# Eight phases of a three-block kernel: where the dense slots lie that TensorE takes ahead across a phase edge

## What is computed

```
x = first_block(x, ...)    # short convolution, sparse attention (16 heads), gated mlp; three gated branches
x = second_block(x, ...)   # stick-breaking, indexed sparse and differential attention; then a feed-forward
x = third_block(x, ...)    # decayed ("forgetting") attention, gated linear recurrence, convolution; feed-forward

g_i = sigmoid(h @ w_in[gate columns i]);  term = g_i * (ys[i] @ w_br[i])      # first block, three branches
p   = masked_softmax(s);  o = p @ v                                            # attention, per head
attn = einsum('bhtk,bhsk,bhtsk->bhts', q, k, decay);  o = attn @ v + (q * exp(b)) @ state   # recurrence, third block
```

## The kernel before

| phase | line | lanes beside the dense one | dense slots, of which led |
|---|---|---|---|
| 1 | 1808 | sparse attention of the first block | 64, 16 |
| 2 | 2781 | stick-breaking attention, key search | 280, 16 |
| 3 | 2792 | head norms, bias tables | 96, 16 |
| 4 | 2819 | attention of the second block | 224, 16 |
| 5 | 2846 | head norm, cuts into halves | 48, 16 |
| 6 | 3564 | recurrence (`Hgrn`) | 96, 16 |
| 7 | 3583 | five norm and gate lanes | 64, 16 |
| 8 | 3607 | attention of the third block, cuts | 56, 16 |

## Time and profile before

### The profile page before, as it was taken

One profiled execution on the slowest core, in us unless ns is written; L12 is line 12 of the kernel. 1 busy time (PEld: TensorE's weight loads), 2 busy tenths in 40 slices (PEclk: granted clock), 3 DMA queues, 4 the chain that ended last, 5 costly groups with the idle time before them and its releaser, 6 DMA issues. The chain is left out here.

```text
span 3029.7 us, 40331 instructions
## 1 busy us (share of the span) xinstructions
PE 2888.8 (95%) x16205; PEld 2351.3 (78%) x16205; DVE 1361.9 (45%) x2458; ACT 1139.7 (38%) x2067; POOL 1237.1 (41%) x593
## 2 busy tenths in 40 slices
PE   6999999999999979999998999999998999999998
PEld 4875557888888867777787999988787757888887
DVE  5427651342043332773542555542477643566620
ACT  4347662222244333443553422222343355432221
POOL 5432214444444532222121545554444422545553
PEclk9989999999999988999997999999999999999999
DMA  7410002222322211113222422223222222422232
GB/s 261 140 49 15 15 29 98 92 97 97 115 94 98 93 47 62 42 42 93 70 84 88 144 85 91 96 98 107 84 92 86 86 73 99 158 95 92 99 102 90
DMA packets 83457, 272.70 MB, mean 90 GB/s; under 512 B 9863, under 2 KB 10119, under 8 KB 83144
## 3 DMA queue, kind: packets, MB, share of 16 engines
q1 hardware_dynamic: 81936, 269.23, 26.9%
q10 hardware_dynamic: 1336, 0.89, 0.1%
HBM read 255.34 MB, written 14.75 MB: 89 GB/s over the span
## 5 line engine op out<-in xcount | busy, mean ns | idle before, releaser
L131 POOL TENSOR_TENSOR weights_lo<-weights_raw,weights_hi 128x1024 fp32r<-128x1024 f32 x415 | 1007.7, 2430 | 1323.9 <-ACT weights_hi L123 1323.7
L123 ACT ACTIVATE weights_hi<-weights_raw 128x1024 fp32r<-128x1024 f32 x415 | 437.7, 1058 | 1049.9 <-PE acc L473 549.1
L471 PE MATMUL acc<-h_hi,weights_hi 128*128 128x512 f32 (+2 forms) x1808 | 665.9, 368 | 25.8 <-POOL h_lo L1350 6.7
L472 PE MATMUL acc<-h_lo,weights_hi 128*128 128x512 f32 (+2 forms) x1808 | 640.0, 354 | 0.0
L473 PE MATMUL acc<-h_hi,weights_lo 128*128 128x512 f32 (+2 forms) x1808 | 639.8, 354 | 0.0
L471 PEld LDWEIGHTS acc<-h_hi,weights_hi 128*128 128x128 f32 x1808 | 346.3, 192 | 106.1 <-issue 52.7
L473 PEld LDWEIGHTS acc<-h_hi,weights_lo 128*128 128x128 f32 x1808 | 346.6, 192 | 45.8
L472 PEld LDWEIGHTS acc<-h_lo,weights_hi 128*128 128x128 f32 x1808 | 347.3, 192 | 41.6 <-issue 0.2
L517 PE MATMUL acc<-weights_hi,h_hi 128*128 128x256 f32 (+1 forms) x480 | 144.8, 302 | 8.0 <-DVE h_lo L979 5.2
L471 PE MATMUL acc<-y_hi,weights_hi 128*128 128x512 f32 (+2 forms) x392 | 142.0, 362 | 10.0 <-DVE full L2725 5.3
L807 ACT ACTIVATE probs<-probs,low 128x31 f32<-128x31 f32 (+5 forms) x276 | 138.5, 503 | 23.1 <-DVE low L774 22.5
(11 more groups left out here) (436 smaller groups left out, 5267.0 us busy)
## 6 DMA issues: line engine op xcount, KB each, us to landing
weights_raw<-in_stream SPq DMA_DIRECT2D x415, 512.0 KB, 3.4
weight_ring<-in_w_ada SPq DMA_DIRECT2D x24, 512.5 KB, 7.5
gates<-gate_tiles SPq DMA_DIRECT2D x24, 258.0 KB, 4.3
gate<-gates SPq DMA_DIRECT2D x8, 774.0 KB, 7.4
held<-gates SPq DMA_DIRECT2D x8, 768.0 KB, 6.4
gates<-gate_tiles SPq DMA_DIRECT2D x23, 256.0 KB, 4.2
flipped<-bias_rows SPq DMA_DIRECT2D x8, 320.0 KB, 4.4
x<-in_x SPq DMA_DIRECT2D x2, 1024.0 KB, 13.9
```

Source lines behind the costliest of these rows:

```text
L123: act.activation(self.hi[:, at % CUT, :], self.raw[:, at % RAW, :], ACT.Copy).then_inc(self.hi_done, 1)
L131: pool.tensor_tensor(self.lo[:, at % CUT, :], self.raw[:, at % RAW, :], self.hi[:, at % CUT, :].bitcast(F32), ALU.subtract).then_inc(self. ...
L471: pe.matmul(out, left[0], right[0], start=start, stop=False)
L472: pe.matmul(out, left[0], right[1], start=False, stop=False)
```

## The change

A new function gives the dense lane a begin below zero, so that the marks of the led slots all lie before 0 and the remaining ones lie evenly from 0 to 1. Eight calls of `paced` use it; nothing else is edited.

```diff
+def ahead(dense, lead):
+
+    first = sum(dense.weights[:lead])
+    return -first / (sum(dense.weights) - first)
...
-            run.lanes(paced((dense.weights, 0, 1), (attention.weights, 0, 1)), [dense, attention], 2 * KT)
+            run.lanes(paced((dense.weights, ahead(dense, 2 * KT), 1), (attention.weights, 0, 1)), [dense, attention], 2 * KT)
...
-                run.lanes(paced((dense.weights, 0, 1), (heads.weights, 0, 1), ([1], 1, 1)), [dense, heads, StoredGates(store)], 2 * KT)
+                run.lanes(paced((dense.weights, ahead(dense, 2 * KT), 1), (heads.weights, 0, 1), ([1], 1, 1)), [dense, heads, StoredGates(store)], 2 * KT)
```

More of the change, by code:

```diff
@@ L2780, in second_attention @@
                 top = TopKeys(sem, sbuf, psum, k, early, penalty)
-                run.lanes(paced((dense.weights, 0, 1), (stick.weights, 0, 1), (top.weights, 0, 1)), [dense, stick, top], 2 * KT)
+                run.lanes(paced((dense.weights, ahead(dense, 2 * KT), 1), (stick.weights, 0, 1), (top.weights, 0, 1)), [dense, stick, top], 2 * KT)
         table = keep("table", [P, 8, TAB])
@@ L2791, in second_attention @@
                             HD, n, w, gains=(bias.scaled, 2))
-            run.lanes(paced((dense.weights, 0, 1), (norm.weights, 0, 1), (bias.weights, 0, 1), ([1], 1, 1)), [dense, norm, bias, StoredGates(store)], 2 * KT)
+            run.lanes(paced((dense.weights, ahead(dense, 2 * KT), 1), (norm.weights, 0, 1), (bias.weights, 0, 1), ([1], 1, 1)), [dense, norm, bias, StoredGates(store)], 2 * KT)
         groups = []
@@ L2818, in second_attention @@
             attention = PairAttend(sem, sbuf, psum, k, groups, True, T2)
-            run.lanes(paced((dense.weights, 0, 1), (attention.weights, 0, 1), ([1], 1, 1)), [dense, attention, StoredGates(store)], 2 * KT)
+            run.lanes(paced((dense.weights, ahead(dense, 2 * KT), 1), (attention.weights, 0, 1), ([1], 1, 1)), [dense, attention, StoredGates(store)], 2 * KT)
 GATES_A, GATES_B, GATES_C = 6, 14, 3
@@ L2845, in second_block @@
             cut = Cut(sem, [(qm[:, t, OUT:], *cuts.tile(t, T_OUT), (lambda act, t=t: act.wait_ge(scaled.done, t - DF_Q + 1)) if t >= DF_Q else None) for t in range(KT)])
-            run.lanes(paced((dense.weights, 0, 1), (scaled.weights, 0, 0.8), (cut.weights, 0, 1), ([1], 1, 1)),
+            run.lanes(paced((dense.weights, ahead(dense, 2 * KT), 1), (scaled.weights, 0, 0.8), (cut.weights, 0, 1), ([1], 1, 1)),
                       [dense, scaled, cut, StoredGates(store)], 2 * KT)
@@ L3582, in third_mixer @@
             gated = GateHeads(sem, hq, silu, both)
-            run.lanes(paced((dense.weights, 0, 1), (forget.weights, 0, 0.8), (fox_norm.weights, 0, 0.9), (head_norm.weights, 0, 0.75),
+            run.lanes(paced((dense.weights, ahead(dense, 2 * KT), 1), (forget.weights, 0, 0.8), (fox_norm.weights, 0, 0.9), (head_norm.weights, 0, 0.75),
                                 (conv_norm.weights, 0, 1), (gated.weights, 0.8, 1), ([1], 1, 1)),
@@ L3606, in third_mixer @@
                       + [(fox[:, FQ + pair, :], *cuts.tile(pair, S), lambda act, pair=pair: act.wait_ge(attention.out_read, len(groups) - pairs + pair + 1)) for pair in range(pairs)])
-            order = paced((dense.weights, 0, 1), (attention.weights, 0, 1), ([1] * (HG + CONV_TILES), 0.2, 0.8), ([1], 1, 1))
+            order = paced((dense.weights, ahead(dense, 2 * KT), 1), (attention.weights, 0, 1), ([1] * (HG + CONV_TILES), 0.2, 0.8), ([1], 1, 1))
             order = [2 if lane == 2 else lane for lane in order]
```

## The result

| | us |
|---|---|
| kernel before, median of 5 runs (range) | 3026.6 (3023.0 to 3031.1) |
| changed kernel, median of 5 runs (range) | 3042.4 (3036.9 to 3045.4) |
| ratio, 95% interval | 1.0054 (1.0043 to 1.0065) |
| profiled execution of the changed kernel, its span | 3043.4, 3041.6 |

The change makes the kernel slower by 16 us (13 to 20 by the interval). The forecast was 3004.0 with a range of 2986 to 3021: wrong in sign, and outside the range.

The account below looks back on a forecast made before the run. TensorE, busy for 2888.8 of 3029.7 us, bounds the kernel; time can come only from its 140.9 idle us or slow work. Eight phase terms sum to -23.0 us: 3026.9 - 23.0 = 3003.9, range 2986 to 3021.

Parts of the forecast that it names:

- rival C: Second half of phase 2: three waits, longer by the thinning, each bring a clock fall; +30 us, 3034 us; chance 0.07.
- rival D: Cover only moves: VectorE and ScalarE pace phases 2, 6, 7, 8, slots go missing later; -0.5 us, 3026 us; chance 0.12.
- Phase 1, -6: Start of phase 1: dense slots in the first gaps keep the clock from falling; -6 us, bounds 0 and 8.5.
- Phase 2, +1: Start of phase 2 gains 1 us, its fall stays; thinner end exposes 2 us of waits; +1, bounds -9 to +4.
- Phase 3, -0.7: Dense slots in phase 3 cover 0.7 of 2.8 us of waits for squares; bounds -2.8 and +1.
- Phase 4, -6.5: Phase 4: three waits of 1.9 us vanish, as does the 10.2 us fall behind them, taken as 4.6; -6.5 us.
- Phase 5, -4: Middle of phase 5: ScalarE's take moves ahead of the norm's chain, seven more slots done, clock still falls; -4 us.
- Phase 6, -2: Phase 6: more dense slots done early gain 5.8 us, later thinning gives back 3.9; -2 us, bounds +2.4 and -5.8.
- Phases 7 and 8, -3 and -1.8: Slots ahead of each item cover waits, 3.5 us for squares and 2.4 for scores, less small losses; -3 and -1.8 us.
- The signs: What would refute the forecast: clocks at 0.50 at phase ends, or phases 2 and 6 growing.

Follow-up runs that it names:

- the best choice of orders alone: Phases 1, 4 and 5 of the kernel before put in the new order, the other five left in the old one; 3018.5 us, ratio 0.9984.

## Why the prediction was wrong

The sum of the eight terms was -23; it came to +12 by the profiles and +16 by the times.

**The failed step** that turned the sign is the same in phases 2, 3 and 6: the thinner cover was priced as waiting time only. For phase 2 the prediction let 2 us of waits appear in the thinner tail and left the clock to fall as it did; for phases 3 and 6 it did not speak of the clock at all. In fact the waits in sum hardly grew (TensorE's idle time even fell by 3.1 us), and what grew is the time at half clock behind them: 47.8 us instead of 27.3 in phase 2, 10.2 instead of 0 in phase 3, 13.7 instead of 6.8 in phase 6. By the means of the profiles, at 0.43 us each, that cost 8.1, 1.8 and 2.5 us. The prediction had the mechanism in hand, in rival C, and gave it 0.07. Its condition, falls as long as the one at the start, was too strict: falls of 3 to 17 us in the second half of the phase were enough, and other phases joined.

**A second step** is as large in sum: gains were counted that did not come or that a later part of the phase took back. From -23 to +12 are 35 us, of which the clock in these three phases makes 12. Phases 4, 5, 7 and 8 make another 15: forecast -15.3, measured +0.1. That cover moved forward is missing later is rival D, which got 0.12; D and C together are what came.

- **Phase 1, -6.** Direction right; -5.2 over all profiles. But it has two parts. The prediction took the fall of 17.0 us in the earlier trace rows, and the slow first round of the earlier trace rows, for a property of the old order. Only two of seven profiles have it: without it the first round ends its last weighing at 217.52 instead of 224.74, and four of seven profiles look so. What the order itself brings is 3.4 us, mostly covered waits (TensorE's idle time 13.5 instead of 16.4), in the middle of the phase and not at its start. That it holds the clock where the old order sometimes does not is right: at most 3.4 us of half clock in six profiles.
- **Phase 2, +1.** Measured +10 to +12, beyond the upper bound of +4. Both parts lose, the new start 7 us and the new tail 3. At the start the prediction counted a microsecond of gain; the waits did shrink from 4.0 to 2.0 us, and the fall grew by 3.4.
- **Phase 3, -0.7** (the heading of that term says -1, the sum takes 0.7). +0.6 without a fall and +5.2 with one. The three waits for squares shrank from 2.8 to 1.8 us as said, but ScalarE's rounding and take delayed its later steps by 3.7 us, and a wait of 2.1 us for the table took the place of one of 0.3. Upper bound +1: missed by the fall.
- **Phase 4, -6.5.** -1.9. The three waits went and the start held its clock in all profiles, as said, but other waits came, and TensorE is idle for 3.3 us instead of 2.8. The rest of the phase gave back some 4 us of the gain. The fall in the tail is not the reason: it is 13.7 or 17.1 us long in the new order and 6.8 to 17.1 in the old one. At an even clock the phase became 1.9 us longer, with five more runs of dense slots; what of it is theirs stays open.
- **Phase 5, -4.** -2.6 in the profile, -1.3 over all, since the old order held its clock for most of the phase once (31.8 us). ScalarE's wait went and one for the norm's low part took its place, as said; it is 2.3 us long, so the clock still fell.
- **Phase 6, -2.** +4.4, beyond +2.4. The first pair product behind the low part came at 2305.79, 17.5 us into the phase, where 16.9 were expected: the rounding, the table load and the exponential lie as worked out. What went wrong comes next. A low part of GpSimd runs beside VectorE and slows it, which the prediction, counting GpSimd's moved steps "at nothing beyond that", had left out:

```profile
2303.80 2.96 POOL L3150 TENSOR_TENSOR k_part<-hf,decay 128x512 f32<-128x512 f32 x2 [0.71 <-ACT decay L3127]
...
2309.36 2.81 POOL L131 TENSOR_TENSOR weights_lo<-weights_raw,weights_hi 128x1024 fp32r<-128x1024 f32 x1
...
2309.88 2.84 DVE L3205 TENSOR_TENSOR kd<-kd,hf 128x512 f32<-128x512 f32 x1
...
2314.14 1.78 PE L3055 MATMUL pair_acc<-q_part,k_part 128*128 128x128 f32 x8 [3.49 <-DVE q_part L3193]
```

These are GpSimd, VectorE and TensorE of the changed kernel in phase 6. The low part that moved ahead of k_part cost nothing (k_part waited for ScalarE's decay). The next one did: the update of kd beside it takes 2.84 us, where it took 0.68, and TensorE waits 3.49. But the kernel before has such a meeting too, later in the chain, where TensorE waited 0.71:

```profile
2308.05 2.56 POOL L131 TENSOR_TENSOR weights_lo<-weights_raw,weights_hi 128x1024 fp32r<-128x1024 f32 x1
...
2308.30 2.86 DVE L3187 TENSOR_TENSOR q_part<-held,decay 128x512 f32<-128x512 f32 x1
```

Over the phase VectorE is busy for 100.5 instead of 97.4 us with the same 140 instructions. How much of the miss this is, no run isolates. The fifth item of the recurrence came 6.4 us later, with 13 slots more done, a gain of 2.6 and not 5.8; the thinner rest then cost 7, where 3.9 was allowed, some 4 of it by 10.2 us at half clock.
- **Phases 7 and 8, -3 and -1.8.** +3.4 and 0. In phase 7 the waits for squares fell from 3.5 to 1.4 us, and a wait of 2.6 us for VectorE appeared at the end, with a fall of 3.4 us behind it. That fall is a small part: with 0 us at half clock and further products the new order still takes 71.8 and 71.9 us, against 70.0. In phase 8 the waits fell by 1.0 us and TensorE, with five more runs of dense slots, was busy for 1.0 us more.
- **The signs.** Those that were to show the prediction wrong ("if clocks at 0.50 appear at phase ends, or if phases 2 and 6 grow") all came.
- **The price of half clock.** The Trainium skill (TensorE: Matmul & The Clock Gate, Terms) takes half of the throttled time; phase 1 gives 7.3 of 17.1 us, 0.43, midway between that and the 6.0 to 17.0 that the prediction preferred. Here the price went from nothing to 0.47, by what else held TensorE up.
- **What makes the clock fall.** Against the rule of long gaps in the Trainium skill (TensorE: Matmul & The Clock Gate, HAM oscillation) the prediction held that waits of half a microsecond suffice. The experiments that kept TensorE busy bear this out for waits of 0.6 to 3.5 us, covered in groups and not one by one. The Trainium skill (TensorE: Matmul & The Clock Gate, A second HAM failure mode: psum-queue depth-cycling) tells of another kernel in which short idle moments between groups of products, frequent enough, made the clock go down and up. This case is near to that, with fewer and longer waits; the prediction did not weigh it.

## What to carry to other kernels

Where the tail of a phase waits for another engine, price a thinner cover in clock, not in idle time alone: the busy total of TensorE at the same instruction count is the sign. A fall read from one profile is an event and not a property; before a forecast rests on it, look for a second profile of the same code. And where a wait can't be covered with work, products of zeros ahead of it cost little: with the old orders they took 17 us off 3026, where the best choice of orders alone took 5.

## What the runs showed of the hardware

- Behind the same wait, in the same code, the clock falls or holds: phase 1 in the old order has 17.1, 6.8 or 0 us at half clock in seven profiles, and the start of phase 2 held once and fell for 23.9 us once with waits of 0.6, 0.5 and 0.7 us and identical instructions in the phase (phase 1 ahead of it differed). The kernel before spreads from 3018 to 3034 us over its runs, and the longest have a lower mean clock (3034.2 us at 0.973, 3031.7 at 0.974; 0.977 or 0.978 in most). (The Trainium skill, TensorE: Matmul & The Clock Gate, Part 1, calls the slow stretch at a kernel's start run-variable; here it holds in its midst.)
- A product of zeros and ones keeps the clock up as well as one of data: phase 2 at 1.00 with either.
- Not every fall follows a wait: in phase 4 of the kernel before the clock fell 146 us into the phase (1601.20), where TensorE had not waited for more than a quarter of a microsecond since the first ten. In the changed kernel it fell there too, 34 us behind a wait of 0.4 us. Why, stays open, as does what ends a fall.
- A microsecond at half clock cost 0.43 to 0.47 us in phases 1, 3 and 6, 0.29 at the start of phase 2, where TensorE also waits for ScalarE, and nothing that shows in phase 7 (70.0 to 70.2 us with 3.4 us of it or none).
- Passing between dense matmuls and other products costs 0.2 to 0.3 us a run in the time of the dense matmuls; TensorE's whole busy time did not fall when runs were joined (153.46 against 153.52 us in phase 4).
- VectorE is slowed beside GpSimd: the same update of kd (128x512) took it 0.68 us alone and 2.84 beside GpSimd's low part.
